# A mixture-of-experts stage with its single big turn paired: turns S, R, Q, P in place of S, P, M, Q, S, and a ring released place by place

## The reference

```python
def swiglu(h, w1, w3, w2):
    return (jax.nn.silu(h @ w1) * (h @ w3)) @ w2

def moe_swiglu(h, router_w, w1, w3, w2):
    logits = (h @ router_w).astype(jnp.float32)
    top_v, top_i = lax.top_k(logits, TOP_K)
    top_p = jax.nn.softmax(top_v, axis=-1)
    comb = jnp.sum(jax.nn.one_hot(top_i, N_EXPERTS, dtype=jnp.float32) * top_p[..., None], axis=-2).astype(h.dtype)
    y = jnp.zeros_like(h)
    for e in range(N_EXPERTS):
        y = y + comb[..., e:e + 1] * swiglu(h, w1[e], w3[e], w2[e])
    return y
```

## Time and profile before

| | |
|---|---|
| runs of the kernel (us) | 1779.04, 1778.52, 1777.74; median 1778.52 |
| the profiled execution (us) | 1777.27 |
| its span in the profile (us) | 1775.2 |
| mean granted TensorE clock | 0.996 |
| TensorE, VectorE, ScalarE busy | 96%, 49%, 39% of the span |
| read from HBM | 477.56 MB, 270 GB/s over the span |

### The profile page before, as it was taken

The page is one execution under the profiler, slowest core; times in us unless marked ns, Lnnn a source line. Parts: engine busy times, 40 slices in busy tenths (PEclk is TensorE's granted clock), DMA queues, the critical chain, the costliest instruction groups (busy, mean ns, idle before and its releaser), DMA issues.

```text
span 1775.2 us, 27608 instructions
## 1 busy us (share of the span) xinstructions
PE 1701.3 (96%) x11166; PEld 1248.7 (70%) x11166; DVE 872.7 (49%) x1209; ACT 691.0 (39%) x900; POOL 50.6 (3%) x62
## 2 busy tenths in 40 slices
PE   6999999999999999999999999998999999998987
PEld 3677677888887789899653577666888887652442
DVE  3435525434533578898420555548987555410001
ACT  4332622222224646654510444536775444300001
POOL 0000000000000022112000000000000000000000
PEclk9999999999999999999999999999999999999999
DMA  9835366433732222231399999999987999999997
GB/s 387 294 134 190 108 214 229 160 92 122 254 97 77 83 84 68 76 108 53 134 410 409 409 409 408 409 409 410 394 323 305 408 407 408 408 409 409 409 408 300
DMA packets 161985, 480.44 MB, mean 271 GB/s; under 512 B 14992, under 2 KB 58176, under 8 KB 155712
## 3 DMA queue, kind: packets, MB, share of 16 engines
q1 hardware_dynamic: 161440, 478.30, 71.0%
q10 hardware_dynamic: 416, 0.36, 0.1%
HBM read 477.56 MB, written 1.05 MB: 270 GB/s over the span
## 4 chain that ended last, share of the span: by engine, by line
PE 71%; DMA 14%; SPq 6%; DVE 4%; ACT 2%; issue 2%; DVEq 0%; ACTq 0%
PE ps L776 17%; PE ps L778 17%; PE ps L777 17%; PE ps L1593 6%; SPq L723 6%; DMA a_slots<-in_moe_w 3%; DMA arena<-in_moe_w 3%; PE ps L1582 3%; DMA raw<-in_moe_up 3%; DMA arena<-in_moe_up 2%; PE ps L795 1%; PE ps L1225 1%; DVE w_lo L2196 1%; PE ps L1664 1%; DMA a_slots<-in_moe_up 1%
## 5 line engine op out<-in xcount | busy, mean ns | idle before, releaser
L2196 DVE TENSOR_TENSOR w_lo<-raw,w_hi 128x1024 fp32r<-128x1024 f32 x220 | 266.2, 1222 | 271.8 <-ACT w_hi L1788 268.8
L1788 ACT ACTIVATE w_hi<-raw 128x1024 fp32r<-128x1024 f32 x220 | 230.4, 1056 | 367.5 <-PE ps L778 296.4
L776 PE MATMUL ps<-h_hi,w_hi 128*128 128x512 f32 (+1 forms) x736 | 279.3, 379 | 3.4 <-DVE h_lo L2278 2.2
L778 PE MATMUL ps<-h_lo,w_hi 128*128 128x512 f32 (+1 forms) x736 | 273.5, 372 | 0.0
L777 PE MATMUL ps<-h_hi,w_lo 128*128 128x512 f32 (+1 forms) x736 | 273.3, 371 | 0.0
L2196 DVE TENSOR_TENSOR w_lo<-arena,w_hi 128x1024 fp32r<-128x1024 f32 x114 | 138.6, 1224 | 91.1 <-ACT w_hi L1788 87.5
L776 PEld LDWEIGHTS ps<-h_hi,w_hi 128*128 128x128 f32 x736 | 138.7, 188 | 48.2 <-issue 23.0
L1788 ACT ACTIVATE w_hi<-arena 128x1024 fp32r<-128x1024 f32 x114 | 120.2, 1060 | 111.5 <-DMA arena<-in_moe_up 55.1
L778 PEld LDWEIGHTS ps<-h_lo,w_hi 128*128 128x128 f32 x736 | 138.7, 188 | 24.4
L777 PEld LDWEIGHTS ps<-h_hi,w_lo 128*128 128x128 f32 x736 | 138.9, 189 | 22.0
L776 PE MATMUL ps<-w_hi,s_parts 128*128 128x512 f32 x336 | 137.2, 408 | 4.1 <-DVE w_lo L2196 4.1
(11 more groups left out here) (398 smaller groups left out, 2456.7 us busy)
## 6 DMA issues: line engine op xcount, KB each, us to landing
arena<-in_moe_up SPq DMA_DIRECT2D x188, 512.0 KB, 14.9
raw<-in_moe_up SPq DMA_DIRECT2D x156, 512.0 KB, 15.0
a_slots<-in_moe_up SPq DMA_DIRECT2D x104, 512.0 KB, 14.8
arena<-in_moe_w SPq DMA_DIRECT2D x98, 512.0 KB, 15.4
raw<-in_moe_w SPq DMA_DIRECT2D x78, 512.0 KB, 15.3
arena<-in_w_ada SPq DMA_DIRECT2D x35, 1024.0 KB, 5.1
raw<-in_ffn_w SPq DMA_DIRECT2D x66, 512.0 KB, 5.8
a_slots<-in_moe_w SPq DMA_DIRECT2D x48, 512.0 KB, 15.3
```

Source lines behind the costliest of these rows:

```text
L776: pe.matmul(dst, s_h, m_h, start=start, stop=False, **kw)
L778: return pe.matmul(dst, s_h, m_l, start=False, stop=stop, **kw)
L1788: act.activation(w_hi[:, o % R, :], src, ACT.Copy).then_inc(hi_done, 1)
L2196: dve.tensor_tensor(w_lo[:, o % R, :], src, w_hi[:, o % R, :].bitcast(F32), ALU.subtract).then_inc(lo_done, 1)
```

## The change

There is no turn M and no fixed S behind Q any more: the fixed turns are `SRQP`. A turn R is a double turn of a big expert and one of 32 places, done as a single strip; the column of the second smallest expert has 32 places now instead of 64. Since double turns now follow one another, TensorE does the four old output steps at places 2, 4, 6 and 8 of a double turn, VectorE at 3, 4, 6 and 7. As the loop's turns know only small outputs, the last double turn's big output is finished ahead of the loop, in PSUM banks 0 to 3. Every small expert's down-projection goes to bank 7 (`S_OUT`). The ring's places 6 to 17 lie elsewhere (`M_AT_COL`, `A_FIRST`), and each waits for its own last reader in place of the common `h_done`. The final transposes use banks 4 and 5 in place of 5 and 7.

```diff
 LOOP_RING = 14
-M_SPACE = 6144
+M_AT_COL = {6: 6144, 7: 7168, 8: 11264, 9: 12288, 10: 13312, 15: 8192, 16: 9216, 17: 10240}
+A_FIRST = 11
...
-KINDS = "SPMQS"
+KINDS = "SRQP"
 FIRST_E = N_EXP - 1
-M_COL = {1: 2, 2: 3, 3: 1}
-S_COL = {0: 0, 1: 5, 3: 7, 4: 6, 5: 4}
-Q_TURN = KINDS.index("Q")
+M_COL = {1: 3, 2: 1, 3: 2}
+S_COL = {0: 0, 1: 6, 2: 7, 3: 5, 4: 4}
+STRIPS = {"Q": (0, 1), "R": (1,)}
+S_OUT = 7
 BOTH = SLOTS + SLOTS // 2
-CAPS = [HALF, SLOTS + QUART, SLOTS, SLOTS, HALF, HALF, HALF, QUART]
...
+            "R": [("m", 0), ("m", 1), ("s", 0), ("s", 1)]}[kind]
+
+
+def strips_of(s):
+
+    return STRIPS.get(KINDS.replace("M", "")[s], ()) if isinstance(s, int) else ()
...
-            for part in {"M": "m", "S": "s", "Q": "bs", "P": "ms"}[kind]:
+            for part in {"M": "m", "S": "s", "Q": "bs", "P": "ms", "R": "ms"}[kind]:
...
+        def ring_slot(k):
+
+            if k < R:
+                return raw[:, k, :]
+            return ar(M_AT_COL[k], UNIT) if k in M_AT_COL else a_slots[:, k - A_FIRST, :]
+
         def moe_slot(n):
...
                     sp.wait_ge(lo_done, u + 1)
+                elif n == R:
+                    sp.wait_ge(r32_done, (NG - 1) * HG)
+                elif n < 10:
+                    sp.wait_ge(o_mm, NG)
+                elif n == 10:
+                    sp.wait_ge(r32_done, HEADS)
+                elif n < A_FIRST + 4:
+                    sp.wait_ge(pe_used, U_MOE)
                 elif n < M_RING:
...
-                    places = {2: (4, 8)}[len(steps)]
+                    places = {2: (4, 8), 4: (2, 4, 6, 8)}[len(steps)]
...
+                        if both:
+                            old_outputs(v + 2)
                         if quart:
...
-                            for q in range(2):
+                            for q in STRIPS[kind]:
                                 for k in range(4):
...
+                            spread_strips(1).then_inc(sx_sp, 1)
...
+                if has_s:
+
+                    pe.wait_ge(sx_spr, tally(s, 1, 1))
...
-                                i = pe.matmul(ps[64 * j:64 * j + 64, 7 if both else 4, :],
+                                i = pe.matmul(ps[64 * j:64 * j + 64, S_OUT, :],
...
+            for half in range(2):
+                yh, yl = y_parts(half)
+                pe.wait_ge(ey_lo, 2 * M_TURNS - 1 + half)
+                for k in range(4):
+                    dst = ps[:, 2 * half + k // 2, k % 2 * 256:k % 2 * 256 + 256]
+                    pe.matmul(dst, yh[:, k * P:(k + 1) * P], spread[:, :], start=True, stop=False)
+                    m = pe.matmul(dst, yl[:, k * P:(k + 1) * P], spread[:, :], start=False, stop=True)
+                m.then_inc(sc_mm, 1)
+
+            pe.wait_ge(acc_rdy, 2 * last + 3)
             with pe.Fori(0, n_loop) as i:
-                moe_turn("S", (i, FIXED), None, (i, S_TURNS), ("S", None, (i, S_TURNS - 1)), (i, last),
+                moe_turn("S", (i, FIXED), None, (i, S_TURNS), ("S", None, (i, S_TURNS - 1)), (i, last + 1),
                          ("S", None, (i, S_TURNS + 1)))
             pe.wait_ge(sx_y, tally((n_loop, S_TURNS - 1), 1, 1))
...
+            out_hi(M_TURNS - 1)
...
-                dve.memset(cap[:, N_EXP - 1:N_EXP], float(QUART))
+                dve.memset(cap[:, N_EXP - 2:N_EXP], float(QUART))
...
-                places = {0: (), 2: (5, 7), 4: (4, 5, 6, 7)}[len(steps)]
+                places = {0: (), 2: (5, 7), 4: (3, 4, 6, 7) if both else (4, 5, 6, 7)}[len(steps)]
...
+            out_scale(M_TURNS - 1)
+            for half in range(2):
+                out_lo(M_TURNS - 1, half)
+            for half in range(2):
+                out_add("m", M_TURNS - 1, half, last, 2 * half)
             with dve.Fori(0, n_loop) as i:
-                moe_turn("S", (i, FIXED), None, (i, S_TURNS), ("S", None, (i, S_TURNS - 1)), (i, last), "S", None,
+                moe_turn("S", (i, FIXED), None, (i, S_TURNS), ("S", None, (i, S_TURNS - 1)), (i, last + 1), "S", None,
                          i + COL_OVER)
             end = (n_loop, S_TURNS - 1)
```

More of the change, by code:

```diff
@@ L209, in alone @@
 def alone(s):
-    pairs = sum(k in "PQ" for k in KINDS)
+    pairs = sum(k in "PQR" for k in KINDS)
     if isinstance(s, tuple):
         return s[0] + (s[1] + 1 - pairs)
-    return s + 1 - sum(k in "PQ" for k in KINDS.replace("M", "")[:s])
+    return s + 1 - sum(k in "PQR" for k in KINDS.replace("M", "")[:s])
 def unit_order():
@@ L246, in splits_by @@
         ahead = v + LEAD + 1
-        if KINDS[tau] in "QP":
+        if KINDS[tau] in "QPR":
             ahead = min(ahead, 4 * (v // 4 + 2))
@@ L1422, in turn_m, with turn_s @@
                 i.then_inc(et_mm, 1)
-            def turn_s(s, cb, bank, adds):
+            def turn_s(s, cb, bank, adds, parts=(0, 1)):
                 pe.wait_ge(sx_hid, tally(s, CB, cb + 1))
@@ L1448, in scatter @@
                     pe.wait_ge(sx_y, tally(n, 1, 1))
-                if kind == "s" and n == s_index(Q_TURN):
+                if kind == "s" and strips_of(n):
+                    strips = strips_of(n)
                     for k in range(4):
@@ L1452, in scatter @@
                         j = (4 * half + k) // 2 * QUART
-                        for q in range(2):
+                        for q in strips:
                             at = X_YS + q * 256 + k % 2 * P
@@ L1602, in moe_turn @@
                         if w == 0 and cb >= 1:
-                            if both and cb == 1 and prev_kind in ("M", "Q", "P"):
+                            if both and cb == 1 and prev_kind in ("M", "Q", "P", "R"):
                                 pe.wait_ge(ey32, prev_m + 1)
@@ L1608, in moe_turn @@
                             if has_s:
-                                turn_s(s, cb - 1, 5 if both else 6, done)
+                                turn_s(s, cb - 1, 5 if both else 6, done, STRIPS.get(kind, (0, 1)))
                     if cb == 2 and has_m:
@@ L1671, in moe_turn @@
                         if has_s:
-                            turn_s(s, CB - 1, 3 if both else 6, done)
+                            turn_s(s, CB - 1, 3 if both else 6, done, STRIPS.get(kind, (0, 1)))
                     if cb == 0 and isinstance(tau, tuple):
@@ L2145, in moe_turn @@
                         if has_s:
-                            turned_s(s, cb, (5, 3)[cb == CB - 1] if both else 6, quart)
+                            turned_s(s, cb, (5, 3)[cb == CB - 1] if both else 6, STRIPS.get(kind))
                     if isinstance(tau, int) and both:
@@ L2805, in out_lo, with out_add @@
                 dve.tensor_tensor(yl, ar(X_Y + half * BANK, BANK), yh.bitcast(F32), ALU.subtract).then_inc(ey_lo, 1)
-            def out_add(what, n, half, adds):
+            def out_add(what, n, half, adds, bank=6):
                 if what == "m":
@@ L2873, in moe_turn @@
                         dve.tensor_copy(cslot_s[:, 0:1], ps[:, 7, 256:257]).then_inc(qx_spr, 1)
-                    if v == (41 if quart else 33 if both else 25) and has_s:
+                    if v == (41 if kind == "Q" else 33 if both else 25) and has_s:
                         at = N_LAT if quart else 0
```

101 lines of the change are left out of this document (52 added, 49 removed).

## The result

| | before | changed |
|---|---|---|
| runs (us) | 1777.74 to 1779.35, 4 runs | 1764.96, 1763.48, 1764.79, 1765.96 |
| median | 1778.78 | **1764.88** |
| profiled execution, its span | 1777.27, 1775.2 | 1764.96, 1763.1 |
| mean granted TensorE clock | 0.996 | 0.986 |

The ratio is 0.9924 (0.9908 to 0.9940): faster by 13.9 us, where 24.8 were forecast, and 1.9 us beyond the upper end of the range. In the profiled executions the difference is 12.3 us.

A forecast was written before the change was run, and what follows sets the result against it. The weight stream at 409 GB/s was taken as the bound wherever TensorE keeps up. Gains 22.2 + 3.1 - 0.5 = 24.8 us gave 1753.7 us; own range 1750 to 1759, 8 in 10 range 1749.5 to 1763.

The forecast's parts named there:

- M's dip: Turn M, 1255 to 1355: stream at 318 instead of 409 GB/s, 22.2 us of transfer time lost, all taken as gained.
- The issues of the first eighteen units: Start of the weight stream: fifteen units issued before 877, three at 877.8, the next near 890.
- the single pass of the loop: Loop runs once, as the rank cut to 32 places has 22 tokens; running twice (1861 us) had chance 0.02.
- The budgets of R, Q and P: Double turns: TensorE alone needs 172, 211 and 214 us, all under the 215.4 us of transfer.
- P's own cost: Old turn P: 215.3 us less 2.7 of waits and 2.9 for the halved clock at its head, 209.7 us.
- the depth of 11.4 us: Ring: how late TensorE may be before the stream runs dry, landing time 15 us less 3.6 for an idle queue.
- the 8 us of old outputs at a turn's head: Heads of double turns: TensorE falls behind by 8 us for old outputs, plus about 3 of late start, covered by depth.
- Rival 2: Heads of Q and P: splits held behind adds stall the ring 10 us each; 1770 to 1779, chance 0.05.
- the start's +3.1: Start: nine places free earlier, nineteenth unit lands at 895.8 instead of 898.9; gain 3.1 us, bounds 0 and 5.3.
- the loop's entry at 0.5: Ahead of the loop: TensorE some 4.2 us later, covered by the ring with 4.0 spare; 0.5 us charged, bounds 0 and 5.
- Rival 1: Turn R: idle gaps halve the clock, R ends 17 us late, some 8 lost; 1759 to 1769, chance 0.16.
- the 1762 that went with this rule: Turn R: if waits for transfers throttle the clock each time, as the skill says, rival 1's case holds in full, 1762 us.

The follow-up runs named there:

- e1: Changed kernel with the old big output's split and VectorE's first two adds moved ahead of the new weights' splits in Q and P; 1758.57 us, ratio 0.9881.
- e10: Changed kernel with the edits of e1, e5 and e7 together, plus filling matmuls before and after the first gather; 1754.62 us, ratio 0.9869.
- e2: Changed kernel with only the old big output's split moved ahead of the new weights' splits, the adds left in place; 1759.12 us, ratio 0.9895.
- e16: Kernel of e10 with the twelve later ring places released together by `h_done` again; 1757.88 us.
- e5: Kernel of e1 with a second turn P (64 places for rank 6 again) in place of R; 1755.57 us, ratio 0.9876.
- e7: Kernel of e1 with the two scatters ahead of the loop in other banks and TensorE's wait for the adds removed; 1755.62 us, ratio 0.9867.
- e8: Kernel of e1 with the twelve later ring places released together by `h_done` again; 1759.86 us, ratio 0.9893.
- e13: Kernel of e9 without the one filling matmul ahead of the first gather; 1759.05 us.
- e4: Changed kernel with ring places 6 to 17 waiting for the common `h_done` again; 1765.59 us, ratio 0.9923.
- e9: Changed kernel with the edits of e1, e5 and e7 together; 1757.46 us, ratio 0.9884.

## Why the prediction was wrong

**Right.** M's dip: the 22.2 us were there to take, and the changed kernel has no stretch like it. The issues of the first eighteen units, the single pass of the loop, the unchanged tail of 10.7 us. The budgets of R, Q and P: with the order mended, the three turns run at 217.4, 218.0 and 217.3 (e1), and with a full P in R's place at 216.2, 218.9 and 216.3 (e10), against 216.2 of pure transfer, so TensorE can keep up. P's own cost was read 0.3 us too low: the earlier trace rows have 6.1 us of matmuls at the halved clock, not 6.4. Q's other 2.7 us are small. A part may be the code: in e10 the queue of instructions moves 0.36 MB during Q and 0.16 during P, and the difference of 0.20 MB is 0.5 us at 409 GB/s. The page's section on queues, for e10 from 1195 to 1411 (packets, MB, share):

```profile
q8 instruction: 22, 0.36, 0.7%
```

and from 1411 to 1627:

```profile
q8 instruction: 10, 0.16, 0.3%
```

The rest is open.

**Wrong, 6.7 us: that the depth of 11.4 us covers "the 8 us of old outputs at a turn's head".** The step that failed is this: the old outputs were costed by their duration on TensorE, and their wait was put at nothing. The split of the old output stood behind splits of units that had not landed. In the kernel before no double turn followed another, so no row of it showed four old outputs at a head. The cover itself was sized rightly: without the wait, in e1, the least time to landing at Q's head is 9.5 us, and the forecast asked for no less than 6; with it, it is 3.5. As a rough sum, 6.5 us of wait, 8 of outputs and some 3 of halved clock exceed 11.4 by about Q's loss of 6.1; P lost 2.2 with nearly the same terms, so the sum is no more than rough. Rival 2 had the place and the other half of the mechanism (splits held behind adds, where outputs were held behind splits; e2's wait of 3.9 us for the first add is the former), 10 us a head where Q lost 6.1 and P 2.2 against 216.2, and a chance of 0.05.

**Wrong, 5.0 us: the start's +3.1, with bounds of 0 and 5.3.** The gain is real: 2.8 to 3.6 us by the landing with the clock full (e10 against e16, e5 to e7 against e8), and against the kernel before the 85th unit then lands 1.7 to 3.4 us earlier (980.2 to 981.9 against 983.6). But the sum took TensorE's start at 889 as given, and "0 (TensorE's start later by as much)" was no lower bound: the clock had held there in the kernel before, with 0.53 us of idle time ahead of the gather, and when it falls, it takes some 4 us (e13 against e10: 3.9), more than the places give. In the profiled run it did, and the term came out at -1.9. A price below nothing should have stood in the range. Nor does the forecast's own range hold the bounds it is said to come from: 1753.7 with no gain at the start and 5 us at the loop's entry is 1761.3, not 1759.

**Off by 1.1 us: the loop's entry at 0.5.** The prediction and the section on the change have TensorE waiting for the first add alone; the wait counts to both (`acc_rdy` of `2 * last + 3`). From the first scatter (1645.8) to the gather (1650.0) it is 4.1 us, not 2.6. The last 84 units took 1.6 us more than before, inside the bounds 0 and 5. But the longer wait is not shown to be the reason: the loads at the entry still took 5.2 us or more to land (6.3 in e1), so the ring covered it, if with less to spare than forecast, and taking the wait out brought nothing with the clock full. Only where the clock halved behind the wait did the last 84 units take up to 7 us more (114.8 in e4).

**Rival 1** was right in kind and wrong in size: eighteen waits for `w_lo` in R, short stretches at 0.50, and at most 1.5 us lost where 17 late at R's end and 8 lost to the stream were feared. The measured time lies inside this rival's 1759 to 1769, but by luck: the loss was at the heads and at the start, not in R. The Trainium skill (TensorE: Matmul & The Clock Gate, "HAM oscillation") says that waits for transfers throttle the clock again and again. The trace agrees that it happens, but not each time: 0.50 at 987.5, 1001.2 and 1195.7 for 3.4 us each, with eighteen waits for `w_lo` in R. That the time came within 3 us of the 1762 that went with this rule is luck too. In R the halved clock costs little; TensorE waits 34.6 us in R in any case, so that it has time to spare against the transfers.

So the time was 11.2 us above the forecast. The two large terms failed in one way: they costed TensorE's work and left out its idle time ahead of it and the clock that this costs. The kernel with the three edits and the fill (e10) lies at 1754.6, ratio 0.9869 (0.9852 to 0.9885), 10 us under the changed one across chips.

## What to carry to other kernels

Where turns follow one another, look at what stands between the finished result and its use in every queue that it passes: here a 1.3 us split stood behind one whose unit landed 5 us later, and TensorE lost those 5 us and the clock after them. Place work whose inputs are there ahead of work that waits for transfers. When TensorE is on the path behind a chain of small steps, its idle time has two prices, the time itself and the halved clock behind it: fill it with matmuls that nobody reads, and put the second price into the range, since it comes in some executions only.

## What was not expected of the hardware

The granted clock fell after only 0.53 us of idle time in five of twelve profiles and not in the others, though TensorE's waits ahead of it were the same to 0.02 us (1.17, 1.17, 0.37, 0.52, 0.19 and 0.53 us from 850 on, in before as in the changed kernel). In four of the five it then stayed at 0.50 for 10.2 us (in the changed kernel with TensorE busy for 9.51 of them), in e9 for 3.4 us. Such falls at the start fit the spread of 4.9 us over the runs of e9 and of 1.8 with the gap filled (e10), but only profiled runs show where the clock fell.
